# Feed-forward zero's last chunk done for both halves as one seven-product pair, with the top-k rounds, query splits and masks placed anew

## The chip, the cores and the metric

The kernel runs on one core of a Trainium2 chip, in one launch. The metric is the device time of an execution in microseconds, the median over runs. The core has five engines that run side by side, each through its own list of instructions in order: TensorE (PE) multiplies matrices, VectorE (DVE) and ScalarE (ACT) work element by element, GpSimd (POOL) too, and SyncE (SP) issues the DMA transfers. They wait for each other through semaphores.

## The reference

Two layers over 1024 tokens of 1024 features, all in float32. `channel_mixer` stands behind each layer and is most of the work:

```python
def dsa_attention(...):              # layer 0, with 8 heads, key and value shared
    score = einsum(wi, relu(qi . ki)); score = where(causal, score, -inf)
    _, idx = lax.top_k(score, 256)   # each query attends to its 256 best keys
    ... softmax(q . k over idx) . v
def even_layer(x): return x + concat([a_out, b_out]) @ w_out            # a_out is the attention
def odd_layer(x):                    # layer 1: conv module
    z = rms_norm(x) @ w_pw1; y = z[..., :1024] * sigmoid(z[..., 1024:])
    y = causal_depthwise_conv(y, w_dw, width=31) + b_dw
    return x + silu(rms_norm(y)) @ w_pw2
def channel_mixer(x, g, w1, w2):     # 1024 -> 4096 -> 1024, behind each layer
    return x + square(relu(rms_norm(x, g) @ w1)) @ w2
```

## The kernel before, in words

Activations lie transposed: 128 features on the partitions, tokens along the free axis. The sequence is worked on in two halves of 512 tokens (`xt0`, `xt1`), so a matmul has a 128x128 weight block and 512 columns. A float32 product is made of three matmuls: both operands are split into a high part (fp32r) and a low part (the rest), and `products` (L916, L917, L918) adds high·high, high·low and low·high in PSUM.

A **unit** is one output tile of 128 features for one half: 8 weight blocks, so 24 matmuls. Its 512 KB of weights are loaded by SP, split by ACT (high part, L1631) and POOL (low part, L1291), three units ahead of PE. `STAGES` is the order of units: the output projection of half 0 (`wout`), feed-forward zero of half 0 (64 units: four chunks of eight up and eight down), the second attention (tiles 4 to 7 of 128 queries) with `wout` of half 1 behind it, pointwise one of half 0, feed-forward zero of half 1 (64 units), pointwise one of half 1, pointwise two and the first chunk of feed-forward one for each half. In an up unit DVE makes relu(psum) times the norm's factor (`relu_scaled`, L2599), ACT squares it into the high part (L1913, L1915), POOL takes the low part (L1437). In a down unit DVE adds the result to x (`add_residual`, L2420).

The other three chunks of feed-forward one run last, in **a paired session**: both halves are one 2x2 block product with the weights, done with seven products in place of eight (`A11, A12, S1, S2, S3, A22, S4`, a scheme of Strassen and Winograd). A product has 4 steps of 12 matmuls (L1265 to L1267). Around them ACT splits weights and activations (`split_weights`, `split_activations`), DVE takes their low parts (`low_weights`, `low_activations`) and forms the sums of blocks that the scheme needs (`sum_weights`, `sum_activations`), and DVE or ACT reads each product out of PSUM (`read_hidden`, `read_output`, `copy_product`). The session's inputs are the two halves normalised (`normalise_inputs`, L2538, L2541), copied ahead by ACT (`keep_second`, L1945).

**Top-k** of a tile is 32 rounds of MAX8 (the eight largest, L2242) and MATCH_REPLACE8 (mark them, L2247) over its scores, on DVE; tile t has 128(t+1) scores a query. Instructions of one tile's rounds wait for each other through `topk_step`; two tiles are interleaved. Tiles (4, 7) are done in the first two chunks of feed-forward zero of half 0, (5, 6) in the last two, one round of both a unit (`more_topk`, L2602). `mask` (L2302) then turns marks into a bias. The second attention has 32 slots (32 to 63), one for each tile and head: PE makes the scores (L1067, L1068), DVE adds the bias and takes the minimum (L2312), ACT the exponential (L1688), PE transposes (L941) and multiplies with the values (L1091). There DVE also splits the next tile's queries (L2271) and makes its mask.

The norm of a stage needs the mean square over all features: ACT squares (L1528), DVE sums and splits the sum, PE multiplies with a matrix of ones (`mean_of`, L929, L930), ACT takes the root, DVE the reciprocal (L2074 to L2076). The taps of the convolution of half 0 run on DVE in 48 units of feed-forward zero of half 1 (`convolve`, L2443).

## Time and profile before

| what | value |
|---|---|
| runs | 2084.3, 2081.86, 2080.52 us; median 2081.86 |
| the profiled execution: its span | 2078.6 us (its own time is given as this span alone) |
| PE busy | 2049.6 us in 9690 matmuls |
| DVE, ACT, POOL busy | 1493.3, 940.3, 938.2 us |
| chain that ended last | PE 87%, DVE 2%, ACT 1% |
| feed-forward zero of half 0 (PE) | from 332.4 to 683.7 |
| second attention, then `wout` of half 1 | to 829.8 |
| pointwise one of half 0, feed-forward zero of half 1 | to 917.5, to 1266.6 |
| paired session at the end | from 1684 to 2075.4 |

The span is from the first to the last instruction that the profiler shows. The page gives busy time for each engine and the chain of waits; windows give it for one stretch; the timeline lists single instructions, with the idle time before each and what ended it in brackets; groups put instructions of one line and shape together.

### The profile page before, as it was taken

The numbers are of one execution on the slowest core, as the hardware profiler recorded it, in microseconds if no ns is written. First come the engines' busy times: TensorE is split into PE (matmuls) and PEld (weight loads), VectorE is DVE, ScalarE is ACT, GpSimd is POOL, SyncE is SP. The second block draws the span as 40 slices with busy tenths as digits, with TensorE's granted clock in tenths as the row PEclk, the third lists the DMA queues.
The fourth block names the chain that finished last, engine by engine and source line by source line (L and its number), as shares of the span: only waits on it lengthen the run. The fifth ranks groups of instructions, "written<-read, shape, count | busy, mean of one in ns | idle before, by whom it ended". The sixth has DMA issues, their size and how long they took to land.

```text
span 2078.6 us, 29271 instructions
## 1 busy us (share of the span) xinstructions
PE 2049.6 (99%) x9690; PEld 1715.7 (83%) x9690; DVE 1493.3 (72%) x2216; ACT 940.3 (45%) x1390; POOL 938.2 (45%) x595
## 2 busy tenths in 40 slices
PE   7999899999999999999999999999999999999999
PEld 7788788888888898888888888888878888888887
DVE  6698758888888443257777634889954587979877
ACT  6644665232323663343323245444365346464562
POOL 5865674554655003556556456857664700000000
PEclk9999999999999999999999999999999999999999
DMA  6321122332323012223233222333353453434433
GB/s 213 93 70 62 45 69 81 104 95 96 102 92 101 11 54 81 92 82 111 92 102 93 100 92 91 103 101 132 122 177 106 162 205 119 162 131 141 148 128 122
DMA packets 77281, 222.62 MB, mean 107 GB/s; under 512 B 7520, under 2 KB 7904, under 8 KB 76128
## 3 DMA queue, kind: packets, MB, share of 16 engines
q1 hardware_dynamic: 73552, 214.60, 31.4%
q10 hardware_dynamic: 3600, 6.32, 0.8%
q8 instruction: 78, 1.28, 0.3%
q14 instruction: 51, 0.42, 0.1%
HBM read 208.31 MB, written 12.58 MB: 106 GB/s over the span
## 4 chain that ended last, share of the span: by engine, by line
PE 87%; DVE 2%; issue 1%; ACT 1%; POOL 0%; DMA 0%; ACTq 0%; DVEq 0%; POOLq 0%
PE psum L916 20%; PE psum L918 20%; PE psum L917 20%; PE psum L1267 6%; PE psum L1266 6%; PE psum L1265 6%; PE psum L1091 3%; PE psum L941 2%; PE psum L1067 1%; PE psum L1068 1%; DVE psum L2443 1%; PE psum L998 0%; POOL w_buf L1291 0%; DMA raw<-weights 0%; PE psum L1008 0%
## 5 line engine op out<-in xcount | busy, mean ns | idle before, releaser
L1291 POOL TENSOR_TENSOR w_buf<-raw,w_buf 128x1024 fp32r<-128x1024 f32 x250 | 607.5, 2431 | 459.8 <-ACT w_buf L1631 438.4
L1631 ACT ACTIVATE w_buf<-raw 128x1024 fp32r<-128x1024 f32 x236 | 248.5, 1054 | 325.7 <-PE psum L918 264.8
L916 PE MATMUL psum<-hid_buf,w_buf 128*128 128x512 f32 x896 | 350.1, 391 | 0.0
L918 PE MATMUL psum<-hid_buf,w_buf 128*128 128x512 f32 x896 | 349.3, 390 | 0.0
L917 PE MATMUL psum<-hid_buf,w_buf 128*128 128x512 f32 x896 | 349.3, 390 | 0.0
L918 PE MATMUL psum<-h_buf,w_buf 128*128 128x512 f32 x896 | 349.1, 390 | 0.0
L916 PE MATMUL psum<-h_buf,w_buf 128*128 128x512 f32 x896 | 349.1, 390 | 0.0
L917 PE MATMUL psum<-h_buf,w_buf 128*128 128x512 f32 x896 | 349.1, 390 | 0.0
L2443 DVE SCALAR_TENSOR_TENSOR psum<-y_buf,wdw,psum 128x512 f32<-128x512 f32 x435 | 295.0, 748 | 0.0
L1265 PE MATMUL psum<-hid_buf,w_buf 128*128 128x512 f32 x576 | 224.4, 390 | 0.0
L1266 PE MATMUL psum<-hid_buf,w_buf 128*128 128x512 f32 x576 | 224.4, 390 | 0.0
L1267 PE MATMUL psum<-hid_buf,w_buf 128*128 128x512 f32 x576 | 224.4, 390 | 0.0
L918 PEld LDWEIGHTS psum<-hid_buf,w_buf 128*128 128x128 f32 x896 | 168.3, 188 | 35.3
L918 PEld LDWEIGHTS psum<-h_buf,w_buf 128*128 128x128 f32 x896 | 168.3, 188 | 34.9
L916 PEld LDWEIGHTS psum<-h_buf,w_buf 128*128 128x128 f32 x896 | 168.3, 188 | 34.8
L917 PEld LDWEIGHTS psum<-h_buf,w_buf 128*128 128x128 f32 x896 | 168.3, 188 | 34.8
L916 PEld LDWEIGHTS psum<-hid_buf,w_buf 128*128 128x128 f32 x896 | 168.4, 188 | 34.6
L917 PEld LDWEIGHTS psum<-hid_buf,w_buf 128*128 128x128 f32 x896 | 168.5, 188 | 34.4
L2420 DVE TENSOR_TENSOR xt<-xt,psum 128x512 f32<-128x512 f32 (+1 forms) x112 | 76.7, 686 | 125.7 <-PE psum L918 124.1
L2247 DVE MATCH_REPLACE8 score<-small,score 128x640 f32<-128x640 f32 (+5 forms) x176 | 158.2, 905 | 0.0
L2242 DVE MAX8 small<-score 128x8 f32<-128x640 f32 (+5 forms) x176 | 153.8, 911 | 2.6 <-ACT b_tok L1583 2.2
L1913 ACT ACTIVATE s_ring<-t_ring 128x512 f32<-128x512 f32 x80 | 50.6, 632 | 226.6 <-DVE t_ring L2599 226.6
(318 smaller groups left out, 3350.4 us busy)
## 6 DMA issues: line engine op xcount, KB each, us to landing
raw<-weights SPq DMA_DIRECT2D x312, 512.0 KB, 3.5
w_more<-weights SPq DMA_DIRECT2D x48, 512.0 KB, 4.3
xt<-x_t SPq DMA_DIRECT2D x2, 2048.0 KB, 8.4
out_t<-xt SPq DMA_DIRECT2D x16, 256.0 KB, 2.0
x_in<-x_t SPq DMA_DIRECT2D x12, 256.0 KB, 6.6
m_kept<-m_ring ACTq DMA_DIRECT2D x12, 256.0 KB, 2.0
c_kept<-c_ring ACTq DMA_DIRECT2D x12, 256.0 KB, 2.7
m_in<-m_kept SPq DMA_DIRECT2D x3, 1024.0 KB, 7.1
```

Source lines behind the costliest of these rows:

```text
L916: nc.tensor.matmul(acc, lhs_hi, rhs_hi, start=first, stop=False)
L917: nc.tensor.matmul(acc, lhs_hi, rhs_lo, start=False, stop=False)
L918: return nc.tensor.matmul(acc, lhs_lo, rhs_hi, start=False, stop=last)
L1265: nc.tensor.matmul(acc, hi, hid_buf[:, 0, k, :], start=start, stop=False, skip_group_check=True)
L1266: nc.tensor.matmul(acc, hi, hid_buf[:, 1, k, :], start=False, stop=False, skip_group_check=True)
L1267: mm = nc.tensor.matmul(acc, lo, hid_buf[:, 0, k, :], start=False, stop=j == 3, skip_group_check=True)
L1291: nc.gpsimd.tensor_tensor(dst_lo, src, dst_hi.bitcast(F32), ALU.subtract).then_inc(done, 1)
L1631: nc.scalar.activation(w_buf[:, 0, :, slot * P:(slot + 1) * P], raw[:, slot % 2], ACT.Copy).then_inc(hi_up, 1)
L2242: V.max(top8[z], score[tiles[z]][:]).then_inc(topk_step, 1)
L2247: V.match_replace(out=s, in_to_replace=top8[z], in_values=s, imm_value=TAKEN).then_inc(topk_step, 1)
L2420: V.tensor_tensor(x, x, psum[:, r, :], ALU.add).then_inc(unit_read, 1)
L2443: ins = V.scalar_tensor_tensor(out=c_buf[:, ct, :] if k == CONV - 1 else acc, in0=yflat(ct, k), scalar=wdw[:, ct, k:k + 1], in1=acc, op0=A ...
```

## The change

The last chunk (q = 3) of feed-forward zero is taken out of both halves' stages (48 units each are left) and done for both halves together in a session of its own, behind `wout` of half 1 and ahead of pointwise one of half 0: 14 products, since all seven are made in the up stage as well. For it the inputs of feed-forward zero are needed twice: x of half 0 is saved to DRAM ahead of that stage and loaded again into `h_first`, x of half 1 is saved ahead of the session and loaded into `h_first` in its last product but a few, as input of feed-forward zero of half 1. The statistics of half 1 are made in the session (`mean_of` at its third step). ACT and DVE make the input of pointwise one in the session's last 14 steps (`early_input`).

Top-k of tiles 4 to 7 gets a new order over 46 units in place of 64: 32 rounds of (4, 5), 19 of (6, 7), 13 of tile 6 alone, spread by their cost. The last 13 rounds of tile 7 (26 steps) go into slots 34 to 54 of the second attention. GpSimd splits the queries and makes the masks of tiles 5 to 7, and DVE waits for the mask at a tile's first head. Half 0's convolution taps start in pointwise one (5 units without, then 3, then 5 a unit) and run at 6 a unit in feed-forward zero of half 1. GpSimd takes the first low parts of the session.

The core of the diff (waits, tiles and SP's loads mostly left out):

```diff
-SOLO = 1
+SOLO0, SOLO = 3, 1
-STAGES = [("wout", 0, WOUT, 8), ("ff0", 0, FF0, 64), ("wout", 1, WOUT, 8), ("pw1", 0, PW1, 16),
-          ("ff0", 1, FF0, 64), ("pw1", 1, PW1, 16),
+STAGES = [("wout", 0, WOUT, 8), ("ff0", 0, FF0, 16 * SOLO0), ("wout", 1, WOUT, 8), ("pw1", 0, PW1, 16),
+          ("ff0", 1, FF0, 16 * SOLO0), ("pw1", 1, PW1, 16),
+ROUNDS_67 = 19
+LATE_GROUPS = [(4, 5)] * ROUNDS + [(6, 7)] * ROUNDS_67 + [(6,)] * (ROUNDS - ROUNDS_67)
+LATE_SLOTS = {**{a: 1 for a in range(34, 55) if a not in (42, 50)}, **{a: 2 for a in (36, 37, 43, 45, 51, 53, 54)}}
+def late_groups_at(u, end):
+    cost = [sum(t + 1.5 for t in tiles) for tiles in LATE_GROUPS]
+    at = [sum(cost[:n + 1]) * end / sum(cost) for n in range(len(cost))]
+    return [tiles for tiles, when in zip(LATE_GROUPS, at) if u < when <= u + 1]
+LATE_STEPS = [(t, take) for tiles in LATE_GROUPS for take in range(2) for t in tiles]
+LATE_STEPS += [(7, take) for _ in range(ROUNDS - ROUNDS_67) for take in range(2)]
 PRODUCTS = [(n, term) for n in range(PAIRED_STAGES) for term in range(TERMS)
+            if n % 2 or n < 2 * EARLY_PAIRS or term not in (A11, A12)]
+EARLY_INPUT_AT = (14, 13, 12, 11, 6, 5, 4, 3)
+PW1_TAPS = ([0] * 5 + [3] * 3 + [5] * 8, [0] * 4 + [4] * 4 + [6] * 8)
+FF0_TAPS = [6] * 16 * (SOLO0 - 1) + [4, 3] + [0] * 14
...
 # TensorE
+            def pair_products(session):
+                for g in range(SESSION[session], SESSION[session + 1]):
+                    v, term, p = g // 4, term_of(g), g % 4
+                    if g == 2:
+                        mean_of("ff0_1", sum_lo)
+                    pe.wait_ge(w_lo, g // 2 + 1)
...
 # GpSimd
+            def split_queries(t):
+                pool.wait_ge(q_split, t)
+                pool.wait_ge(tr_up, TR["q", t - 1, 1] + 1)
+                stack, q = stack_of(t), q_tok[:, t]
+                link(nc.gpsimd.tensor_scalar(q, q, -(HD ** -0.5), None, ALU.mult))
+                link(nc.gpsimd.tensor_copy(stack[:, :, 0, :], q))
+                T(stack[:, :, 1, :], q, stack[:, :, 0, :].bitcast(F32), ALU.subtract).then_inc(q_split, 1)
+            def mask(t):
+                pool.wait_ge(topk_step, late_steps_through(t))
+                nc.gpsimd.tensor_scalar(score[t][:], score[t][:], 0.9 * TAKEN, -NEG, ALU.is_gt, ALU.mult
+                                        ).then_inc(late_mask, 1)
+                elif (name, half) == ("wout", 1):
+                    for t in range(5, 8):
+                        split_queries(t)
+                        mask(t)
+                    units(first, 8, last=True)
+                    for m in range(3):
+                        first_low_weights(m)
+                    for z in range(2):
+                        first_low_activations(1, z)
+                    first_low_weights(3)
...
 # ScalarE
-                    units(first, 8, again(0, "pw1_0", G_OD, h_buf))
+                    units(first, 8, both(square_second(first), keep_second(G_FF0), split_first), last=True, unrolled=True)
+                    pair_splits(0)
+            def split_first(i, r):
+                if i and r % 2:
+                    split_activations(0, r // 2)
+            def pair_splits(session):
+                first, end = SESSION[session], SESSION[session + 1]
+                for m in range(first // 2, first // 2 + W_AHEAD // 2):
+                    split_weights(m)
+                    if session == 0 and m:
+                        split_activations(1, m - 1)
...
 # VectorE
+            def late_topk(count):
+                for n in range(late_done[0], late_done[0] + count):
+                    t, take = LATE_STEPS[n]
+                    before, s = late_step_before(n), score[t][:]
+                    wait_apart(dve, topk_step, STEPS_01 + (0 if before is None else before + 1), passed_v)
+                    if take:
+                        ins = V.match_replace(out=s, in_to_replace=top8[t % 2], in_values=s, imm_value=TAKEN)
+                    else:
+                        ins = V.max(top8[t % 2], s)
+                    ins.then_inc(topk_step, 1)
+                late_done[0] += count
 # in attention_slot
+                if t > 4 and h == 0:
+                    dve.wait_ge(late_mask, t - 4)
+                if a in LATE_SLOTS:
+                    late_topk(LATE_SLOTS[a])
 # in feed-forward zero of half 0
+                            for tiles in late_groups_at(u, 16 * SOLO0 - 2):
+                                late_topk(2 * len(tiles))
+                            if u == 16 * SOLO0 - 2:
+                                mask(4)
+                                attention_slot(32, 1)
+            def early_input(k):
+                n = KT * PREP["pw1_0"] + k
+                prep_low(n, k, flat(xt[0], None, k), h_buf, G_OD)
+                add_squares(KT * SUM["pw1_0"] + k, k % 2, sq_sum[:])
+            def pair_sums(session):
+                first, end = SESSION[session], SESSION[session + 1]
+                if session == 0:
+                    split_sums("ff0_1")
+                    norm_of("ff0_1", rms_second)
+                    for k in range(4):
+                        normalise_second(k, rms_second)
+                for g in range(first, end):
+                    v, p = g // 4 + 1, g % 4
+                    if session == 0 and g in (5, 6):
+                        normalise_second(2 * g - 6, rms_second)
+                        normalise_second(2 * g - 5, rms_second)
...
```

## Rows read from the trace of the kernel before

**Rows 1.** The page: busy time of each engine; the chain by engine

```profile
PE 2049.6 (99%) x9690; PEld 1715.7 (83%) x9690; DVE 1493.3 (72%) x2216; ACT 940.3 (45%) x1390; POOL 938.2 (45%) x595
...
PE 87%; DVE 2%; issue 1%; ACT 1%; POOL 0%; DMA 0%; ACTq 0%; DVEq 0%; POOLq 0%
```

**Rows 2.** Windows: us, busy PE, PEld, DVE, ACT, POOL; clock, DMA share, GB/s

```profile
427.00:514.00 87.00, 87.00 (x386) 72.12 (x385) 73.25 (x114) 26.24 (x32) 48.48 (x24) 1.00 0.30 97
683.70:783.80 100.10, 98.56 (x784) 92.70 (x783) 44.28 (x86) 65.85 (x139) 0.00 (x0) 1.00 0.08 29
```

**Rows 3.** Timeline, PE and DVE, first units of feed-forward zero: start, duration

```profile
332.43 0.40 PE L916 MATMUL psum<-h_buf,w_buf 128*128 128x512 f32 x1
...
344.49 0.69 DVE L2599 SCALAR_TENSOR_TENSOR t_ring<-psum,rms_bc 128x512 f32<-128x512 f32 x1 [0.33 <-DVE rms_bc L2076]
...
348.94 0.68 DVE L2599 SCALAR_TENSOR_TENSOR t_ring<-psum,rms_bc 128x512 f32<-128x512 f32 x1
```

**Rows 4.** Groups by shape, top-k on DVE: busy us, mean ns, idle

```profile
L2242 DVE MAX8 small<-score 128x8 f32<-128x1024 f32 x32 | 38.7, 1209 | 0.0
L2242 DVE MAX8 small<-score 128x8 f32<-128x896 f32 x32 | 34.4, 1075 | 0.0
L2242 DVE MAX8 small<-score 128x8 f32<-128x768 f32 x32 | 30.4, 950 | 0.0
L2242 DVE MAX8 small<-score 128x8 f32<-128x640 f32 x32 | 26.2, 819 | 0.0
```

**Rows 5.** Timeline, last relu of an up stage to its low part

```profile
426.51 0.69 DVE L2599 SCALAR_TENSOR_TENSOR t_ring<-psum,rms_bc 128x512 f32<-128x512 f32 x1 [0.79 <-PE psum L918]
...
428.99 1.30 POOL L1437 TENSOR_TENSOR hid_buf<-s_ring,hid_buf 128x512 f32 x1 [4.37 <-ACT hid_buf L1915]
```

**Rows 6.** Timeline, DVE: one round of tile 3 alone

```profile
209.06 0.68 DVE L2242 MAX8 small<-score 128x8 f32<-128x512 f32 x1
...
210.78 0.69 DVE L2242 MAX8 small<-score 128x8 f32<-128x512 f32 x1
```

**Rows 7.** Timeline, DVE, end of feed-forward zero; group of ACT's exponentials

```profile
677.57 0.69 DVE L2420 TENSOR_TENSOR xt<-xt,psum 128x512 f32<-128x512 f32 x1 [0.91 <-PE psum L918]
678.18 0.49 DVE L2302 TENSOR_SCALAR score<-score 128x640 f32<-128x640 f32 x1
...
L1688 ACT ACTIVATE p_buf<-s_buf,small 128x640 f32<-128x640 f32 x8 | 6.6, 828 | 5.5 <-DVE small L2312 5.1 <-PE psum L941 0.3
```

**Rows 8.** Second attention, L2312 on DVE: a slot; idle before it, times

```profile
698.68 0.82 DVE L2312 CUSTOM_DVE_ANT_0 s_buf<-psum,score 128x640 f32<-128x640 f32 x1 [1.53 <-PE psum L1068]
...
  PE psum L1068: 42.8, 24
```

**Rows 9.** Groups by shape: ACT's squares and weight splits, POOL's low parts

```profile
L1528 ACT ACTIVATE sq_ring<-xt 128x512 f32<-128x512 f32 x24 | 14.8, 617 | 0.0
L1631 ACT ACTIVATE w_buf<-raw 128x1024 fp32r<-128x1024 f32 x236 | 248.5, 1054 | 325.7 <-PE psum L918 264.8 <-DMA raw<-weights 34.4 <-DVE m_ring L2561 16.7
L1291 POOL TENSOR_TENSOR w_buf<-raw,w_buf 128x1024 fp32r<-128x1024 f32 x250 | 607.5, 2431 | 459.8 <-ACT w_buf L1631 438.4 <-ACT w_buf L1538 20.3 <-POOL q_tok L1318 0.5
```

**Rows 10.** Timeline, PE: from the output projection into pointwise one

```profile
829.54 0.39 PE L918 MATMUL psum<-hid_buf,w_buf 128*128 128x512 f32 x1
829.76 0.39 PE L916 MATMUL psum<-h_buf,w_buf 128*128 128x512 f32 x1
```

**Rows 11.** Timeline, DVE and POOL: half 1 normalised, beside weight splits

```profile
1640.86 10.41 DVE L2538 TENSOR_TENSOR h_second<-h_second,rms_bc 128x512 f32<-128x512 f32 x8
...
1644.46 5.65 POOL L1291 TENSOR_TENSOR w_buf<-raw,w_buf 128x1024 fp32r<-128x1024 f32 x2
```

**Rows 12.** Timeline, PE: the first matmuls after a long stop

```profile
10.79 0.69 PE L916 MATMUL psum<-hid_buf,h_buf 128*128 128x424 f32 x1 [7.58 <-DVE h_buf L2088]
...
14.11 0.43 PE L916 MATMUL psum<-hid_buf,h_buf 128*128 128x424 f32 x1
...
14.57 0.36 PE L918 MATMUL psum<-hid_buf,h_buf 128*128 128x424 f32 x1
```

More of the change, by code:

```diff
@@ L506, in build @@
         x_kept = nc.dram_tensor("x_kept", (P, KT, HALF), F32)
+        x_early = [nc.dram_tensor(f"x_early{half}", (P, KT, HALF), F32) for half in range(2)]
         m1_kept = nc.dram_tensor("m1_kept", (P, 4 * PRE, HALF), F32)
@@ L1182, in mlp @@
                     if q == 0:
-                        units(first, 8, operand, prep_lo, KT * PREP[name], mean=(name, sum_lo))
+                        units(first, 8, operand, prep_lo, KT * PREP[name],
+                              mean=None if (stage, half) == ("ff0", 1) else (name, sum_lo))
                     else:
@@ L1194, in mlp @@
                     mean = None
-                    if q == 3 and (stage, half) == ("ff0", 1):
+                    if q == chunks_of(stage)[-1] and (stage, half) == ("ff0", 1):
                         mean = ("conv0", sum_lo)
@@ L1922, in mlp @@
                         continue
-                    if q == 3 and (stage, half) == ("ff0", 1):
+                    if q == chunks_of(stage)[-1] and (stage, half) == ("ff0", 1):
                         squares = conv_squares(0)
-                    units(first + 16 * q, 8, both(hidden_hi, squares), mean=None if q else name_of(stage, half))
+                    units(first + 16 * q, 8, both(hidden_hi, squares), unrolled=squares is not None,
+                          mean=None if q or (stage, half) == ("ff0", 1) else name_of(stage, half))
                     if (stage, half) == ("ff1", 1):
@@ L2618, in mlp @@
                         continue
-                    if conv and not late and q < 3:
+                    if (stage, half) == ("ff0", 0):
+                        residual = add_residual(down, half)
                         for r in range(16):
-                            done = 16 * q + r
+                            u = 16 * q + r
+                            if u == 16 * SOLO0 - 8:
+                                split_queries(4)
                             if r < 8:
@@ L2641, in mlp @@
                             clear_sum(psum[:, 7, :])
-                        if (stage, half) == ("ff0", 0):
-                            split_queries(4)
-                            residual, rounds = add_residual(down, half), more_topk(1)
-                            units(down, 4, residual, rounds)
-                            for r in range(4):
-                                residual(1, r)
-                                if r < 2:
-                                    rounds(1, r)
-                                if r == 2:
-                                    mask(4)
-                                    attention_slot(32, 1)
-                            continue
                         if (stage, half) == ("ff1", 1):
```

618 lines of the change are left out of this document (381 added, 237 removed).

## The prediction, made before the change was run

> **What bounds the kernel now.** I read the page first: TensorE (PE) is busy 99% of the span and holds 87% of the chain that ended last [rows 1], so time leaves the kernel only with matmuls, and enters it wherever PE is made to wait. Then the windows by stage: in a stretch of feed-forward zero PE works without a gap and a matmul costs 87.00/386 = 0.2254 us, while VectorE (DVE) is busy 84% of it, with top-k rounds; in the second attention DVE is busy 44% [rows 2]. Last the timelines at the places where the change puts a new chain in front of PE. Each instruction's own time comes from the groups by shape.
>
> **PE's matmuls.** The last chunk of feed-forward zero costs 2 halves × 16 units × 24 = 768 matmuls before, and 14 products × 4 steps × 12 = 672 as a pair. 96 × 0.2254 = **−21.6**. Everything below is what has to be paid for it.
>
> **First chunk of feed-forward zero, half 0.** DVE starts its first relu 12.1 us after PE's first matmul of the stage (344.49 against 332.43) [rows 3]. Before, relu and a (4,7) round take 348.94 − 344.49 = 4.45 of a unit's 24 × 0.2265 = 5.44 us, so DVE gains 1 us a unit on PE. The round's share is 4.45 − 0.61 = 3.84, against 2 × (0.819 + 1.209) = 4.06 of the four instructions [rows 3, 4]: interleaved rounds run at 0.946 of their sum. After, the first 23 units hold 32 rounds of (4,5): 2 × (0.819 + 0.950) × 0.946 = 3.35 each, 1.39 a unit, with the relu 5.3 of 5.44. The backlog hardly drains. At the turn from the up to the down matmuls DVE is about 2.5 late; the chain from the last relu to the low part of the hidden tile takes 430.29 − 426.51 = 3.78 [rows 5], and the last tile is wanted 7 × 3 × 0.2265 = 4.76 after the turn. 2.5 + 3.78 − 4.76 = **+1.5** (0 if the backlog drains as before, 4 if it doesn't at all). Later turns find it smaller.
>
> **Tail of that stage.** Units 40 to 45 hold one (6,7) round, 13 rounds of tile 6 alone, and 6 relu or residual steps. A lone round is a chain: MAX8, MATCH_REPLACE8, MAX8 on one score tile. The one such row is tile 3, 512 wide: 210.78 − 209.06 = 1.72, where two instructions at the interleaved rate would be 2 × 0.680 × 0.946 = 1.29 [rows 4, 6]. So +0.43 of waiting a round, and tile 6 alone costs 2 × 1.075 × 0.946 + 0.43 = 2.46. 13 × 2.46 + 4.32 + 6 × 0.61 + 1.4 (splitting queries of tile 4) = 41.4. DVE can't begin with them before PE ends unit 40, 41 × 5.44 = 223.0 into the stage, so it is done at 264.4. (Over the whole stage: 12.1 + 32 × 3.35 + 19 × 4.32 + 13 × 2.46 + 46 × 0.61 + 1.4 = 263, about the same: there is no slack left anywhere.) Behind that stand unit 46's residual 0.61, mask 0.5 and masked minimum 0.82, then ScalarE's exponential 0.83 and 0.1 for hops [rows 7, 8], before PE may go on with slot 32's probabilities: 267.3, where its units end at 48 × 5.44 = 261.1. **+6.1** (0 to 8: nothing if lone rounds run at the interleaved rate; 8 if the first chunk's backlog is still there).
> Here the Trainium skill speaks against me: "VectorE: DVE Perf Modes", section "The DRAIN you can't avoid", says that the pipeline is emptied after each VectorE instruction anyway and that a semaphore between chained ones costs nothing extra. By it this term would be 0.5. The row shows otherwise, so the rule is only a rival.
>
> **Second attention.** 13 rounds of tile 7, lone too, are 26 steps of 1.21 = 31.5 us [rows 4], in slots 34 to 54. DVE waits there 42.8 us for scores, 24 times [rows 8]: 1.8 a slot. A slot with one step fits. Seven slots have two, 2.42, of which some 0.85 goes past the wait; the slots' probabilities lie about 0.4 ahead of PE. I take 0.3 for each of seven, **+2.0** (0 to 6, all of 7 × 0.85). GpSimd's splits and masks are off DVE there. Its mask of 1024 has no row; bounds are DVE's own of 640, 0.49 [rows 7], and GpSimd's two-input subtraction of 1024, 2.43 [rows 9]; I take 1.6 (one input), and even 2.43 with the split before it fits the two slots (6 us) between tile 7's last step and its first masked minimum. So zero; were it late, DVE would stand at a tile's first minimum, and everything of that slot behind it.
>
> **Start of the paired chunk.** Before, PE passes from the output projection into the next stage without a gap (829.54, 829.76) [rows 10], since the weights of the next units were split ahead. After, ScalarE first ends the last unit's work: residual 0.69 on DVE, square 0.617 and a scaled copy of the same size; then half of the first activations 1.054, the first weights' high part 1.054, and GpSimd's low part 2.43 [rows 7, 9], with hops of 0.3 in all: **+6.8** of PE standing (5.5 if the copy falls behind the split, 7.5 with longer hops).
>
> **S1, the third product.** Its right-hand side needs half 1 normalised. The mean can only be made after PE's first two steps (5.4 into the session), then root and norm, 4 normalisations of the second half, the subtraction and its two splits, all in DVE's order among its weight sums. The eight normalisations in the row took 10.41/8 = 1.30 each, beside GpSimd's subtraction, where DVE's residual of the same size takes 0.69 [rows 7, 11]. That order puts the low part of S1's second half about 36.3 after the projection's end; PE wants it at 6.8 + 8 steps × 2.72 + half a step 1.36 + the mean's own matmuls 0.4 = 30.3. In two waits (2.2 and 3.9) **+6.1** (0 if the statistics come as early as the weights, 3.3 without GpSimd's hold on DVE, 9 if sums wait too).
>
> **End of the paired chunk.** The input of pointwise one is made in its last 14 steps; DVE gets 8 subtractions and 8 sums more there and is about 0.8 late for the last reads: **+0.8** (0 to 3). Pointwise one starts with three weight units split ahead, so no gap there. Feed-forward zero of half 1 gets six taps a unit, 6 × 0.69 + 0.61 = 4.7 of 5.44: zero. The 2 MB moves lie on SyncE's queue in front of weight units that have two slots of slack: zero; were one late, it would show as a wait of ScalarE for a load.
>
> **Clock.** The granted clock is 1.00 in every stretch [rows 2], the higher of the two levels (1.2 and 2.4 GHz). After PE stood 7.58 us early in the kernel, nine matmuls of 424 columns took 14.11 − 10.79 = 3.32, 0.37 each, and the next two 14.57 − 14.11 = 0.46, 0.23 each [rows 12]: about 9 × 0.14 = 1.3 us at the lower level. The new stop of 6.8 can bring one such; **+1.0** (0 to 5: three more stops).
>
> **Sum:** −21.6 + 1.5 + 6.1 + 2.0 + 6.8 + 6.1 + 0.8 + 1.0 = +2.7. From the profiled span of 2078.6, 2081.3; the runs' median, 2081.86, lies 3.3 above that span, so 2084.6, told as 2084.5. This kernel's measurement can tell 0.2%, 4.2 us, from no change; +2.7 is inside it.
>
> **Rivals.**
> *Lone rounds cost no more than interleaved ones.* For it: the row of a lone round is one of few, of another tile, and from a stretch with other work. Against: 1.72 beside 1.29 [rows 6]. The tail's 6.1 falls by 13 × 0.43 = 5.6, and 2084.5 to 2079. (The Trainium skill's section on the DRAIN, named above, says this.)
> *DVE keeps up.* The (4,5) backlog drains, the tail fits, and S1's operands come in time: for it, DVE is idle 16% of the stage's stretch [rows 2], and half of the normalisations may run beside an idle GpSimd at 0.69 rather than 1.30. Against: the two sums over units above. −21.6 + 0 + 1 + 1 + 6.8 + 2 + 0.8 + 0 = −10, so 2072.
> *The second attention becomes DVE's* (the other side). Place: slots 34 to 54. A slot's steps stand behind its minimum and in front of the next one; where a step isn't ready (it waits for the one before it, lone) or a slot is shorter than 0.82 + 1.21 and PE's 0.4 of lead is used up, each of 19 slots pays: 7 × 0.85 + 12 × 0.2 = 8.4 rather than 2.0. It decides from the first slot whose scores PE must hold back. For it: tile 4's slots come every 1.53 + 0.82 = 2.35 us [rows 8], and one step leaves 0.3 of that. Against: 42.8 of waiting for 31.5 of work. 2091.
>
> **Chances.** The forecast .42, its own range 2078 to 2088 (.34 of it within 0.2%, .08 slower); lone rounds free .10 (half within, half faster); DVE keeps up .20 (faster); the second attention, or as many repeated cold starts, .28 (slower). Faster .25, same .39, slower .36. The range 2071 to 2094 holds all four cases' middles and leaves the joint extremes out.
>
> **What would show it.** In the profile after: 96 matmuls fewer at an unchanged pitch; DVE idle almost nowhere between 345 and 590; a PE gap near 6 us before slot 32's values, ended by an exponential; a gap near 7 us between the projection and the first paired matmul, ended by GpSimd's weights; two gaps before S1, ended by VectorE; a few slots of under 1 us. I am wrong if DVE idles in the tail, if PE reaches S1 later than its operands, or if PE waits in a stage that I put at zero (pointwise one's start, half 1's feed-forward zero).

## The result, and the profile after

The changed kernel takes 2087.4 us (median of 11 runs, 2085.6 to 2089.1), the kernel before 2081.7 (11 runs): a ratio of 1.0028, 95% interval 1.0020 to 1.0036. It is slower by 5.7 us, more than the 0.2% from which the forecast told a change. The forecast was 2084.5, in the range 2071 to 2094.

The page of the changed kernel, busy time by engine:

```profile
PE 2040.1 (98%) x9594; PEld 1704.9 (82%) x9594; DVE 1603.8 (77%) x2314; ACT 972.0 (47%) x1420; POOL 876.0 (42%) x565
```

9690 − 9594 = 96 matmuls are gone, as computed, and with them 21.8 us of PE's time at the pitch of 0.2267 (a unit of 24 in 5.44); but its busy time falls by only 9.5 [rows 1], and beside it stand stops. The stops, from the timeline of PE (start, duration, in brackets the idle time and what ended it):

```profile
602.40 0.76 PE L1069 MATMUL psum<-ident,p_buf 128*128 128x128 f32 x5 [3.48 <-ACT p_buf L1865]
676.47 0.95 PE L1069 MATMUL psum<-ident,p_buf 128*128 128x128 f32 x7 [0.69 <-ACT p_buf L1865]
759.19 0.80 PE L1376 MATMUL psum<-b_first,w_buf 128*128 128x512 f32 x1 [6.66 <-POOL w_buf L1561]
788.57 0.80 PE L1376 MATMUL psum<-hid_buf,w_buf 128*128 128x512 f32 x1 [3.12 <-DVE hid_buf L2712]
901.28 0.50 PE L1376 MATMUL psum<-hid_buf,w_buf 128*128 128x512 f32 x1 [2.23 <-DVE hid_buf L2712]
1016.71 0.70 PE L1044 MATMUL psum<-hid_buf,w_buf 128*128 128x512 f32 x1 [2.43 <-DVE hid_buf L2303]
```

In order: slot 32's probabilities (the tail), tile 7's first slot, the start of the paired chunk, S1, A22 at the end of the chunk, and the first unit of half 1's feed-forward zero. "Half clock" below is time at the lower of the two levels. Where the kernel before has no gap at all [rows 10], there are 6.66 us. The second half of the loss is not idle time. Windows of the changed kernel (columns as in [rows 2]), first a full-speed stretch, then those behind five of the stops:

```profile
466.00:509.00 43.00, 43.00 (x192) 35.59 (x191) 40.98 (x59) 9.88 (x11) 23.71 (x11) 1.00 0.31 98
602.40:612.00 9.60, 9.44 (x45) 8.50 (x45) 5.99 (x12) 4.32 (x11) 0.78 (x1) 0.64 0.01 3
759.20:764.00 4.80, 4.80 (x11) 3.80 (x12) 0.00 (x0) 2.14 (x3) 4.80 (x3) 0.50 0.53 167
788.60:792.00 3.40, 3.40 (x9) 2.74 (x10) 3.40 (x5) 0.52 (x1) 0.00 (x0) 0.57 0.04 11
901.30:906.00 4.70, 4.70 (x21) 3.88 (x22) 4.08 (x5) 1.81 (x2) 0.00 (x0) 1.00 0.08 30
1016.70:1021.00 4.30, 4.29 (x12) 3.38 (x13) 4.27 (x8) 0.74 (x1) 2.38 (x1) 0.60 0.01 4
```

PE is busy the whole of each stretch, with half as many matmuls as time: 11 in 4.80 us behind the start's stop, at a granted clock of 0.50 (the 1.2 GHz level), where 4.80/0.2267 = 21 fit at 2.4 GHz. Time lost is the stretch times one minus the clock: 3.5 + 2.4 + 1.5 + 1.7 = 9.1 us.

The account of this execution: −21.8 + stops (3.5 + 0.7 + 6.7 + 3.1 + 2.2 + 2.4 = 18.6) + half clock 9.1 = +5.9, beside +5.7 between the medians. The smaller stops nearly cancel: over these stages they add up to 1.8 here, and the kernel before stood 2.1 there. This execution is the slowest of the eleven; its span, 2087.3, lies 8.7 above the profiled 2078.6, of which 2.3 is there when feed-forward zero starts (334.70 below, 332.43 in [rows 3]), so 6.4 is to be set beside the 5.9.

Readings that the steps below need, from the timeline of the changed kernel. PE's first matmul of feed-forward zero, then lone rounds of tile 6 and VectorE's minimum of slot 32:

```profile
334.70 0.40 PE L1044 MATMUL psum<-h_buf,w_buf 128*128 128x512 f32 x1
...
592.05 1.09 DVE L2465 MAX8 small<-score 128x8 f32<-128x896 f32 x1
593.29 0.09 DVE L2463 MATCH_VALUE_LOAD score<-small,score 128x8 f32 x1 [0.15 <-DVE small L2465]
593.37 1.07 DVE L2463 MATCH_REPLACE8 score<-small,score 128x896 f32<-128x896 f32 x1
594.59 1.09 DVE L2465 MAX8 small<-score 128x8 f32<-128x896 f32 x1
...
600.56 0.82 DVE L2543 CUSTOM_DVE_ANT_0 s_buf<-psum,score 128x640 f32<-128x640 f32 x1
```

A lone round takes 594.59 − 592.05 = 2.54, with waits of 0.15 between its steps; the minimum stands 265.9 behind PE's first matmul. The first turn of that stage from up to down units (PE's first down matmul, VectorE's last relu, GpSimd's last low part):

```profile
379.53 0.39 PE L1044 MATMUL psum<-hid_buf,w_buf 128*128 128x512 f32 x1
...
380.43 0.68 DVE L2845 SCALAR_TENSOR_TENSOR t_ring<-psum,rms_bc 128x512 f32<-128x512 f32 x1
...
382.74 1.29 POOL L1603 TENSOR_TENSOR hid_buf<-s_ring,hid_buf 128x512 f32 x1 [0.24 <-ACT hid_buf L2089]
```

Two units of pointwise one on VectorE, from one read of PSUM to the next but one:

```profile
989.73 0.68 DVE L3037 TENSOR_TENSOR s_ring<-psum,rms_bc 128x512 f32<-128x512 f32 x1
991.73 1.39 DVE L2303 SCALAR_TENSOR_TENSOR hid_buf<-h_first,gain,hid_buf 128x512 fp32r<-128x512 f32 x1 [1.31 <-ACT hid_buf L1699]
...
1001.51 0.68 DVE L3037 TENSOR_TENSOR s_ring<-psum,rms_bc 128x512 f32<-128x512 f32 x1
```

And GpSimd's mask of tile 7, with VectorE waiting for it:

```profile
669.53 3.65 POOL L1556 TENSOR_SCALAR score<-score 128x1024 f32<-128x1024 f32 x1 [26.23 <-DVE score L2463]
...
673.34 1.22 DVE L2543 CUSTOM_DVE_ANT_0 s_buf<-psum,score 128x1024 f32<-128x1024 f32 x1 [2.90 <-POOL score L1556]
```

### The profile page after: what moved, and what is told of

Same layout as the page of the kernel before. It is cut to its first block, busy times and chain, and to the rows that moved or that the text cites. A ratio compares the mean times of both kernels' runs of the same rounds, so it can differ in the third digit from the quotient of the medians.

```text
span 2087.3 us, 28431 instructions
## 1 busy us (share of the span) xinstructions
PE 2040.1 (98%) x9594; PEld 1704.9 (82%) x9594; DVE 1603.8 (77%) x2314; ACT 972.0 (47%) x1420; POOL 876.0 (42%) x565
## 3 DMA queue, kind: packets, MB, share of 16 engines
q8 instruction: 77, 1.26, 0.2%
## 4 chain that ended last, share of the span: by engine, by line
PE 53%; DVE 3%; issue 1%; ACT 0%; DMA 0%; POOL 0%; ACTq 0%; DVEq 0%
PE psum L1044 11%; PE psum L1046 11%; PE psum L1045 11%; PE psum L1378 7%; PE psum L1376 7%; PE psum L1377 7%; DVE psum L2679 1%; DVE hid_buf L2303 1%; PE psum L1343 0%; PE psum L1345 0%; PE psum L1347 0%; DVE psum L2696 0%; DMA raw<-weights 0%; ACT hid_buf L1699 0%; DVE s_ring L3037 0%
## 5 line engine op out<-in xcount | busy, mean ns | idle before, releaser
L1433 POOL TENSOR_TENSOR w_buf<-raw,w_buf 128x1024 fp32r<-128x1024 f32 x218 | 529.4, 2431 | 483.2 <-ACT w_buf L1808 461.3
L1808 ACT ACTIVATE w_buf<-raw 128x1024 fp32r<-128x1024 f32 x204 | 214.5, 1053 | 246.5 <-PE psum L1046 179.9
L1376 PE MATMUL psum<-hid_buf,w_buf 128*128 128x512 f32 x784 | 305.9, 390 | 5.4 <-DVE hid_buf L2712 5.4
L1378 PE MATMUL psum<-hid_buf,w_buf 128*128 128x512 f32 x784 | 305.5, 390 | 0.0
L1377 PE MATMUL psum<-hid_buf,w_buf 128*128 128x512 f32 x784 | 305.5, 390 | 0.0
L1044 PE MATMUL psum<-hid_buf,w_buf 128*128 128x512 f32 x768 | 300.6, 391 | 2.4 <-DVE hid_buf L2303 2.4
L1045 PE MATMUL psum<-hid_buf,w_buf 128*128 128x512 f32 x768 | 299.7, 390 | 0.0
L1046 PE MATMUL psum<-hid_buf,w_buf 128*128 128x512 f32 x768 | 299.6, 390 | 0.0
L1046 PE MATMUL psum<-h_buf,w_buf 128*128 128x512 f32 x768 | 298.8, 389 | 0.0
L1044 PE MATMUL psum<-h_buf,w_buf 128*128 128x512 f32 x768 | 298.8, 389 | 0.0
L1045 PE MATMUL psum<-h_buf,w_buf 128*128 128x512 f32 x768 | 298.8, 389 | 0.0
L1376 PEld LDWEIGHTS psum<-hid_buf,w_buf 128*128 128x128 f32 x784 | 147.5, 188 | 36.7 <-DVE hid_buf L2712 6.2
L1377 PEld LDWEIGHTS psum<-hid_buf,w_buf 128*128 128x128 f32 x784 | 147.6, 188 | 30.9
L1378 PEld LDWEIGHTS psum<-hid_buf,w_buf 128*128 128x128 f32 x784 | 147.4, 188 | 30.6
L1044 PEld LDWEIGHTS psum<-hid_buf,w_buf 128*128 128x128 f32 x768 | 144.6, 188 | 32.7 <-DVE hid_buf L2303 2.9
L1046 PEld LDWEIGHTS psum<-hid_buf,w_buf 128*128 128x128 f32 x768 | 144.6, 188 | 30.6
L1045 PEld LDWEIGHTS psum<-hid_buf,w_buf 128*128 128x128 f32 x768 | 144.7, 188 | 29.8
L1044 PEld LDWEIGHTS psum<-h_buf,w_buf 128*128 128x128 f32 x768 | 144.1, 188 | 30.1
L1046 PEld LDWEIGHTS psum<-h_buf,w_buf 128*128 128x128 f32 x768 | 144.2, 188 | 30.0
L1045 PEld LDWEIGHTS psum<-h_buf,w_buf 128*128 128x128 f32 x768 | 144.1, 188 | 29.9
L2463 DVE MATCH_REPLACE8 score<-small,score 128x640 f32<-128x640 f32 (+3 forms) x128 | 128.4, 1010 | 0.0
```

The costliest lines, as they stand in the source:

```text
L1044: nc.tensor.matmul(acc, lhs_hi, rhs_hi, start=first, stop=False)
L1045: nc.tensor.matmul(acc, lhs_hi, rhs_lo, start=False, stop=False)
L1046: return nc.tensor.matmul(acc, lhs_lo, rhs_hi, start=False, stop=last)
L1376: nc.tensor.matmul(acc, hi, b_split(v, 0, j), start=start, stop=False, skip_group_check=True)
L1377: nc.tensor.matmul(acc, hi, b_split(v, 1, j), start=False, stop=False, skip_group_check=True)
L1378: mm = nc.tensor.matmul(acc, lo, b_split(v, 0, j), start=False, stop=j == 3, skip_group_check=True)
```

## The experiments

Each was timed against the kernel before in the same session, with 5 to 11 runs; ratios are to that kernel, with a 95% interval. Times are to be held against 2087.4.

**e_mean: the statistics of half 1 earlier.** On PE and on ScalarE:

```diff
-                    if g == 2:
+                    if g == 0:
                         mean_of("ff0_1", sum_lo)      # and root_of on ScalarE
```

> The changed kernel, but with the mean of half 1 (TensorE) and its root (ScalarE) ahead of the paired chunk's first step and not of its third. Theory (the stop before S1 hangs on the statistics, which wait for TensorE's own third step while VectorE stands still for 9 us): the stop of 3.3 us before S1 goes, and with it the half clock of the eight matmuls behind it, 1.7: 2087.4 - 5.0 = 2082.4. Rival (VectorE's order of weight sums and splits ahead of S1 decides): the stop stays at 2 to 3, and the time at 2086 to 2087.

2085.7 (1.0019, 1.0010 to 1.0028). The stop before S1 stays at 2.75, so the theory fell, though not for the rival's reason. VectorE, GpSimd and PE's stop before S1 in this run's timeline:

```profile
763.63 8.41 DVE L2771 TENSOR_TENSOR h_second<-h_second,rms_second 128x512 f32<-128x512 f32 x4
...
762.87 5.21 POOL L1566 TENSOR_TENSOR hid_buf<-h_first,hid_buf 128x1024 fp32r<-128x1024 f32 x2
768.03 2.85 POOL L1561 TENSOR_TENSOR w_buf<-w_more,w_buf 128x1024 fp32r<-128x1024 f32 x1
...
787.19 0.78 PE L1376 MATMUL psum<-hid_buf,w_buf 128*128 128x512 f32 x1 [2.75 <-DVE hid_buf L2712]
```

and in the changed kernel:

```profile
770.62 2.80 DVE L2771 TENSOR_TENSOR h_second<-h_second,rms_second 128x512 f32<-128x512 f32 x4
...
763.77 4.92 POOL L1566 TENSOR_TENSOR hid_buf<-h_first,hid_buf 128x1024 fp32r<-128x1024 f32 x2
768.66 2.40 POOL L1561 TENSOR_TENSOR w_buf<-w_more,w_buf 128x1024 fp32r<-128x1024 f32 x1
```

The normalisations begin 7 us earlier (1 of it this execution's own, as the start's stop ends at 758.1 for 759.2) and take 8.41 in place of 2.80: they end at 772.0, 1.2 behind GpSimd's last low part, and in the changed kernel at 773.4. What was won ahead was lost beside GpSimd. Counted from the end of the output projection, PE goes on with S1 after 35.57 (787.19 − 751.62) in this run and after 36.04 (788.57 − 752.53) in the changed kernel.

**e_port: the six first low parts on VectorE.** e_mean, and

```diff
                     units(first, 8, last=True)            # GpSimd
-                    for m in range(3):
-                        first_low_weights(m)
-                    for z in range(2):
-                        first_low_activations(1, z)
-                    first_low_weights(3)
...
                     split_sums("ff0_1")                   # VectorE
+                    low_weights(0)
+                    for z in range(2):
+                        low_weights(1 + z)
+                        low_activations(1, z)
                     norm_of("ff0_1", rms_second)
...
-                        if g > 1:
-                            low_weights((g - 1 + W_AHEAD) // 2)
+                        low_weights((g - 1 + W_AHEAD) // 2)
```

> The changed kernel with the mean of half 1 ahead of the first step, as in the run before with the early mean (2085.7; there four normalisations took 8.41 us beside GpSimd's low parts, where they had taken 2.80 after them), and besides VectorE makes the paired chunk's six first low parts in place of GpSimd. Theory (GpSimd's low parts hold VectorE's two-input instructions until they are done, 20 us after the projection's end, and so decide when S1's operands come): four normalisations take 2.8, the stop before S1 (3.1 to 3.3) goes with the half clock behind it: 2087.4 - 5.0 = 2082.4; TensorE's stop at the start stays near 6.9. Rival (VectorE's own work decides; it gets 6 x 1.2 = 7.3 us more): the stop before S1 stays at 2 or more, 2086 to 2088.

2081.5 (0.9999, 0.9990 to 1.0008). VectorE's normalisations, and PE's stops before S1 and in S2:

```profile
764.09 2.50 DVE L2766 TENSOR_TENSOR h_second<-h_second,rms_second 128x512 f32<-128x512 f32 x4
...
783.15 0.50 PE L1376 MATMUL psum<-hid_buf,w_buf 128*128 128x512 f32 x1 [0.38 <-DVE hid_buf L2707]
...
795.31 0.50 PE L1376 MATMUL psum<-hid_buf,w_buf 128*128 128x512 f32 x1 [0.99 <-DVE hid_buf L2707]
```

2.50 for four, although they start at the same point as in e_mean; what is gone beside them is GpSimd. VectorE has 7.3 us more to do, and S1's stop falls from 2.75 in e_mean to 0.38 (a new one of 0.99 in S2 stands beside that); no half clock follows them. PE goes on with S1 33.29 behind the projection's end. This is shown, since the two runs differ only in the engine that makes them: GpSimd's low parts set when S1's operands come. By the Trainium skill's "SBUF — State Buffer", section "Who interferes with whom", a VectorE instruction with two inputs in SBUF contends with a GpSimd instruction that reads SBUF; 8.41 beside 2.50 agrees.

**e_start: the first splits ahead of the projection's last unit.**

```diff
-                if i and r % 2:
-                    split_activations(0, r // 2)
+                if i and r in (1, 2):
+                    split_activations(0, r - 1)
+                if i and r == 2:
+                    split_weights(0)
+                    split_weights(1)
...
+                    if session or m > 1:
                         split_weights(m)
...
-                        if m >= 6:
-                            low_activations(0, m - 6)
+                        if m == 6:
+                            low_activations(0, 0)
+                            low_activations(0, 1)
```

> The changed kernel, but ScalarE splits the first two weight pairs and the first activations ahead of its work on the projection's last unit, so that the low parts are ready when the projection ends. Theory (the stops add up, since the statistics of half 1 hang on TensorE's own third step and move with it): the stop of 6.8 at the start of the paired chunk falls under 1 and the half clock behind it (2.6) goes; S1's stop stays near 3.3: 2087.4 - 9 = 2078. Rival (S1's operands are bound to the projection's end, whenever TensorE starts): the stop before S1 grows by what the start gave, to 9 or 10, and only 1 to 3 us are won: 2085.

2081.9 (1.0004, 0.9995 to 1.0013): 5.5 of the 9 that adding up would give. PE's stops, and VectorE's normalisations:

```profile
750.63 0.50 PE L1376 MATMUL psum<-b_first,w_buf 128*128 128x512 f32 x1 [1.26 <-POOL w_buf L1561]
...
760.01 5.42 DVE L2775 TENSOR_TENSOR h_second<-h_second,rms_second 128x512 f32<-128x512 f32 x4
...
775.47 0.76 PE L1376 MATMUL psum<-hid_buf,w_buf 128*128 128x512 f32 x1 [2.30 <-DVE hid_buf L2716]
...
780.59 0.50 PE L1376 MATMUL psum<-hid_buf,w_buf 128*128 128x512 f32 x1 [2.22 <-DVE hid_buf L2716]
```

The start's stop falls from 6.66 to 1.26, the two before S1 grow from 3.12 to 4.52. Both theories hold in part: about a quarter of the win comes back.

**e_warm: matmuls in the stop.** It adds 28 matmuls, whose result the next product overwrites.

```diff
+                    if g == 0:
+                        pe.wait_ge(unit_read, UNITS_BEFORE[0] - 3)
+                        pe.wait_ge(b_hi, 1)
+                        for _ in range(28):
+                            nc.tensor.matmul(product_bank(0), b_first[:, 0, 0, 0:P], b_first[:, 0, 0, :], start=True,
+                                             stop=True, skip_group_check=True)
```

> The changed kernel, with 28 matmuls more, of 512 columns, written to a PSUM bank that the next product overwrites, in TensorE's stop between projection and paired chunk. They take 6.3 us of the 6.8 and nothing waits for them. Theory (the twelve matmuls behind the stop at 0.43 us, at a granted clock of 0.50, are real time): the granted clock there is 1.00, the time 2087.4 - 2.6 = 2084.8. Rival (S1's stop is bound to the projection's end and takes up what the clock gives): clock 1.00, but S1's stop grows by 1 to 2.6 and the time stays within 1 us of 2087.4.

2087.3 (1.0029, 1.0018 to 1.0039): no change, the rival's figure. The window behind the start; the projection's last matmul and PE's stops before S1; VectorE's normalisations:

```profile
758.30:763.00 4.70, 4.61 (x20) 3.84 (x21) 0.00 (x0) 3.72 (x5) 4.70 (x3) 1.00 0.57 159
```

```profile
751.27 0.39 PE L1046 MATMUL psum<-hid_buf,w_buf 128*128 128x512 f32 x1
...
782.56 0.47 PE L1382 MATMUL psum<-hid_buf,w_buf 128*128 128x512 f32 x1 [1.63 <-DVE hid_buf L2718]
...
787.68 0.79 PE L1382 MATMUL psum<-hid_buf,w_buf 128*128 128x512 f32 x1 [3.49 <-DVE hid_buf L2718]
...
767.47 5.07 DVE L2777 TENSOR_TENSOR h_second<-h_second,rms_second 128x512 f32<-128x512 f32 x4
```

20 matmuls in place of 11, clock 1.00: with PE kept at work there is no half clock. The 2.4 us come back before S1, whose stops grow from 3.12 to 5.12. In the changed kernel the half clock at the start was therefore free: S1 would have waited anyway. PE goes on with S1 787.68 − 751.66 = 36.02 behind the projection's end, as in the changed kernel (36.04): the normalisations begin 2.3 earlier, counted from there, and take 5.07 in place of 2.80.

**e_taps: eight taps later.**

```diff
-PW1_TAPS = ([0] * 5 + [3] * 3 + [5] * 8, ...)
-FF0_TAPS = [6] * 16 * (SOLO0 - 1) + [4, 3] + [0] * 14
+PW1_TAPS = ([0] * 5 + [3] * 3 + [4] * 8, ...)
+FF0_TAPS = [6] * 16 * (SOLO0 - 1) + [6, 6, 3] + [0] * 13
```

> The changed kernel, but eight convolution taps moved from pointwise one's last eight units (4 a unit in place of 5) to the end of half 1's feed-forward zero. Theory: the stop of 2.6 us in the first unit of that feed-forward, where the eighth normalised tile is late behind five taps, goes, and so does the half clock behind it (nine matmuls, 2.0): 2087.4 - 4.6 = 2082.8. If the half clock in the rows costs no time: 2084.8. Rival (the taps only carry the lateness to the last chunk): 2087.

2083.2 (1.0008, 0.9999 to 1.0017), −4.2, near the theory with the half clock counted. The window of that stage's first units, without a stop, and from the changed kernel one of the subtractions that its taps stood beside:

```profile
1005.00:1020.00 15.00, 15.00 (x68) 12.43 (x67) 12.72 (x18) 4.53 (x6) 7.91 (x5) 1.00 0.34 107
```

```profile
1008.72 1.37 DVE L2303 SCALAR_TENSOR_TENSOR hid_buf<-h_first,gain,hid_buf 128x512 fp32r<-128x512 f32 x1
```

**e_end: pointwise one's input later.**

```diff
-EARLY_INPUT_AT = (14, 13, 12, 11, 6, 5, 4, 3)
+EARLY_INPUT_AT = (10, 9, 8, 7, 6, 5, 4, 3)
```

> The changed kernel with the first four tiles of pointwise one's input made 10 to 7 steps ahead of the paired chunk's end and not 14 to 11. Theory (the stop of 2.4 us before A22, the last product but one, comes from these subtractions and sums standing in VectorE's queue ahead of A22's low parts): it goes, 2087.4 - 2.4 = 2085, or 2084 where a half clock followed it. Rival (VectorE is full over the whole stretch): the stop only moves, before S4 or into pointwise one, 2087.

2083.3 (1.0009, 1.0000 to 1.0018), −4.1: the stop before A22 is gone, and no other comes between it and pointwise one. It gave more than the 2.2 of the stop; behind that same stop the profiles of e_mean, e_start, e_taps, e_bal and f_session show clocks of 0.59 to 0.64 over 4 to 5 us, those of the changed kernel, e_warm, e_port and e_dve 1.00, so a half clock in some executions is the likely rest; it is not shown.

**e_bal: fewer lone rounds.** 5 rounds of tile 6 and 9 of tile 7 in the second attention, 4 lone ones ahead of it.

```diff
-ROUNDS_67 = 19
-LATE_GROUPS = [(4, 5)] * ROUNDS + [(6, 7)] * ROUNDS_67 + [(6,)] * (ROUNDS - ROUNDS_67)
-LATE_SLOTS = {**{a: 1 for a in range(34, 55) if a not in (42, 50)}, **{a: 2 for a in (36, 37, 43, 45, 51, 53, 54)}}
+ROUNDS_67, LATE_6 = 23, 5
+LATE_GROUPS = [(4, 5)] * ROUNDS + [(6, 7)] * ROUNDS_67 + [(6,)] * (ROUNDS - ROUNDS_67 - LATE_6)
+LATE_SLOTS = {**{a: 1 for a in range(33, 55)}, **{a: 2 for a in (43, 45, 47, 51, 53, 54)}}
+LATE_STEPS += [(6, take) for _ in range(LATE_6) for take in range(2)]
```

> The changed kernel with another split of the top-k rounds: 32 rounds of (4,5), 23 of (6,7) and only 4 of tile 6 alone in feed-forward zero of half 0, and in the second attention 5 rounds of tile 6 and 9 of tile 7 (28 steps for 26). VectorE's work in feed-forward zero falls by 13 x 2.5 + 19 x 4.3 - 4 x 2.5 - 23 x 4.3 = 5 us. Theory (the stop of 3.6 us before slot 32's values is VectorE's lateness, and the half clock in the slots behind it, 0.65 over 10 us, costs about 3): the stop falls under 0.5, the slots run at full clock: 2087.4 - 6 = 2081. Rival (the second attention then becomes VectorE's, with two more steps and no free slot): the stop goes, but its slots lose 3 to 6 us: 2084 to 2087.

2087.2 (1.0029, 1.0018 to 1.0039): no change. PE's stops at the tail and three slots on:

```profile
597.93 0.76 PE L1070 MATMUL psum<-ident,p_buf 128*128 128x128 f32 x5 [1.23 <-ACT p_buf L1866]
605.29 0.33 PE L1070 MATMUL psum<-ident,p_buf 128*128 128x128 f32 x1 [1.62 <-ACT pt_buf L1815]
```

The tail falls from 3.48 to 1.23, and the clock behind it is 1.00, but slots that had none now stop. PE's stops up to tile 7's first slot add up to 5.5 in this profile and 5.4 in the changed kernel: what the tail gave, the slots took, as the rival said. That the half clock's 3.5 doesn't show in the median either stays open. In this profile some of it came back elsewhere: over the 10 us behind S1's stop the clock was 0.72 (0.85 in the changed kernel), over the 10 us behind A22's 0.83 (1.00).

**e_dve: queries and masks back on VectorE.**

```diff
-                    for t in range(5, 8):                # GpSimd
-                        split_queries(t)
-                        mask(t)
...
-                if t > 4 and h == 0:                     # VectorE
-                    dve.wait_ge(late_mask, t - 4)
-                if h == Q_AT - 3 and t < 3:
+                if h == Q_AT - 3 and t % 4 < 3:
                     split_queries(t + 1)
-                if h == 7 and t < 3:
+                if h == 7 and t % 4 < 3:
                     mask(t + 1)
```

> The changed kernel with the queries of tiles 5 to 7 split and their masks made by VectorE, in the slots where the kernel before did it, and not by GpSimd. It adds three times some 1.4 + 0.6 = 6 us to VectorE in the second attention. Theory (VectorE's late rounds leave little there): the slots lose 2 to 5 us, 2089 to 2092. Rival (42.8 us of idle time for 31.5 us of steps leave room): within 1 us of 2087.4, and GpSimd's part of the change was worth nothing.

2092.2 (1.0049, 1.0035 to 1.0062): +4.8, as the theory had it. GpSimd's part is worth it in spite of its slow mask. In the profiles PE needs 153.47 from slot 32's values to the projection's end, for 150.13 in the changed kernel, with 996 matmuls in both: it stands 3.1 for 2.0, and is busy 150.4 for 148.1, so two thirds of the loss here are half clock and not waiting.

**f_session, f_most, f_all, f_last: toward a version that beats both.** f_session has e_start's splits, `low_weights(0)` on VectorE behind them and the other first low parts there ahead of the norm, with PE's mean where it was and ScalarE's root a step earlier:

```diff
+                            low_weights(0)               # at m == 6
...
+                    for z in range(2):                   # behind split_sums
+                        low_weights(1 + z)
+                        low_activations(1, z)
+                    low_weights(3)
```

> The run with VectorE making the first low parts (2081.5), and besides the early first splits (alone 2081.9): first two weight pairs and first activations split by ScalarE ahead of the projection's last unit, their low parts made by VectorE there, the mean again ahead of the third step, the root a step earlier on ScalarE. Theory (the start's stop and S1's are both bound to the projection's end by the same chain of first low parts; off GpSimd it is short enough for both): start under 0.5, S1's stops under 2 in all, no half clock: 2087.4 - 6.8 - 2.6 - 2.5 = 2075.5. Rival (VectorE's own chain binds S1 to the projection's end): what the start gives, up to 6.4, comes back before S1: 2080 to 2082.

2080.1 (0.9992, 0.9983 to 1.0001). The start's stop is 0.1, but S1's are 1.43 and 3.49: nearest to the rival. f_most adds e_taps and e_end:

> The run before, and with it the taps moved (alone 2083.2, -4.2) and pointwise one's input made later (alone 2083.3, -4.1). Theory (the stops lie in different stages and add up): 2075.5 - 8.3 = 2067, 14 under the kernel before. Rival (the median is not a sum of stops; part of the half clock counted in each is one execution's chance): 2070 to 2072.

2074.4 (0.9962, 0.9949 to 0.9976), −5.7 and not −8.3. f_all moves 3 rounds of tile 6 into the second attention, in exchange for 3 of tile 7:

```diff
+ROUNDS_67, LATE_6 = 22, 3
```

> The run before, and with it 22 rounds of (6,7), 7 of tile 6 alone, and in the second attention 3 rounds of tile 6 and 10 of tile 7: the same 26 steps in the same slots as the change, 1.9 us less of VectorE ahead of slot 32. Theory: the stop of 3.6 before slot 32's values falls to 1.7 and the half clock behind it (about 3) goes in most executions: 2 to 5 under the run before. Rival (as with 28 steps: what the stop gives, the slots lose): within 1 us of the run before.

2072.8 (0.9958, 0.9944 to 0.9971), no change that can be told from f_most. The theory failed: the stop before slot 32's values is 3.32, for 3.47 in f_most.

```profile
599.97 1.33 PE L1070 MATMUL psum<-ident,p_buf 128*128 128x128 f32 x5 [3.32 <-ACT p_buf L1861]
```

f_last puts S1's two low parts one behind the other:

```diff
+                        if g == 5:
+                            low_activations(v, 0)
+                            low_activations(v, 1)
+                            dve.wait_ge(product_up, g + 1)
+                            read_hidden(g)
...
-                    if session == 0 and g in (5, 6):
+                    if session == 0 and g in (7, 8):
                         normalise_second(...)
```

> The fastest run so far (2072.8), with VectorE's order ahead of S1 changed: both low parts of S1's activations one behind the other, then the read of the sixth product step, and the last four normalisations of half 1 (2 x 1.28 us) only behind them, where S2's sums need them. Theory (the two stops left before S1, 1.6 and 3.7, are VectorE's order: 5 us of other work between its two low parts): both fall under 1 and the half clock behind them goes: 2072.8 - 4 to - 6 = 2067 to 2069. Rival (VectorE is full from the projection's end to S2, so what is put off is late there): the stops move to S1's later steps or to S2: within 1.5 us of 2072.8.

2070.8 (0.9949, 0.9935 to 0.9962), the fastest, though its interval overlaps that of f_all: 16.6 under the change, 10.8 under the kernel before. Two windows of the paired chunk, and the stops that are left in the second:

```profile
740.00:775.00 35.00, 34.64 (x152) 28.02 (x151) 30.69 (x35) 18.02 (x22) 0.00 (x0) 1.00 0.51 180
775.00:800.00 25.00, 20.78 (x90) 16.30 (x89) 23.52 (x23) 18.06 (x24) 0.00 (x0) 1.00 0.41 138
```

```profile
784.21 0.47 PE L1377 MATMUL psum<-hid_buf,w_buf 128*128 128x512 f32 x1 [2.28 <-DVE hid_buf L2712]
...
787.53 0.50 PE L1377 MATMUL psum<-hid_buf,w_buf 128*128 128x512 f32 x1 [1.71 <-DVE hid_buf L2712]
```

The start and S1 run through; VectorE, busy 23.52 of 25.00, is late for S2 now. What is put off there is late there, as the rival said, but less: S1's 4.9 (1.44 and 3.49 in f_all) are gone and S2's 4.0 came. Its clock was 1.00 behind all of its stops, the tail's 3.33 too, which no other profile with a tail above 3 shows; so a part of the 2.0 under f_all may be this execution's chance.

## Why the prediction was right or wrong

The range held the time and the sign of the sum was right; its size was half the measured one, by terms that miss in both directions: together they were 8.5 too high (first chunk, tail, second attention, start, S1) and 11.9 too low (end of the chunk, pointwise one, clock). That the time came out within 3 us is in part luck.

| term | forecast | profile after |
|---|---|---|
| 96 matmuls | −21.6 | −21.8 |
| first chunk | +1.5 | 0 |
| tail | +6.1 | 3.5 |
| second attention | +2.0 | 0.7 |
| start | +6.8 | 6.7 |
| S1 | +6.1 | 3.1 |
| end of the chunk | +0.8 | 2.2 |
| pointwise one into half 1 | 0 | 2.4 |
| half clock | +1.0 | 9.1 |

- **Clock: the step that failed.** "The new stop of 6.8 can bring one such" counted one restart, of 1.3 us. Four of six stops had one. The one behind S1's stop (9 matmuls in 3.40, 1.5 lost) was like the row; the other three cost 1.7, 2.4 and 3.5, and what makes them longer is not shown. My bound of 5 was too low as well. But the 9.1 isn't all a loss that mending brings back: e_warm shows that the start's 2.4 is paid by S1's wait either way.
- **96 matmuls:** the count was right; 87.00/386 takes in the matmuls that the window's edges cut, so the pitch of 0.2254 was 0.5% short.
- **Start:** right, by its own chain, down to the releaser (GpSimd's low part).
- **Tail:** VectorE came when forecast: its minimum 265.9 after PE's first matmul of the stage, where the sum had 264.4 + 0.61 + 0.5 = 265.5, and PE went on 267.7 after it, for 267.3. The lone round was 2.54 against 2.46, so the row of tile 3 carried over. The stop was 3.5 and not 6.1 because PE's side of the subtraction was too small: 48 × 5.44 left out the mean, the transposes of tile 4's queries and slot 32's scores, some 3 us. f_all adds that the order counts and not the stage's total: with 1.9 us less of work on VectorE the last three units still held two, two and three lone rounds, as in f_most, and the stop stayed. The Trainium skill ("VectorE: DVE Perf Modes", section "The DRAIN you can't avoid") measured that a semaphore after each of a row of VectorE copies costs nothing extra. If that held here, a lone round would take 2 × 1.075 × 0.946 = 2.03, an estimate; the trace's 2.54 is against it: a step that waits for the one before it starts 0.15 after its end, while interleaved rounds run at 0.946 of their sum [rows 3, 4].
- **First chunk:** no stop, by a narrow margin. VectorE's last relu began 0.90 behind the turn (380.43 − 379.53) and not 2.5; its low part was done at 4.50 (382.74 + 1.29 − 379.53), wanted at 4.76. The 2.5 had no working, and the sum's own numbers give more: 12.1 + 7 × 5.27 = 49.0, where the turn is at 8 × 5.44 = 43.5. Measured, the last relu stood 45.7 behind PE's first matmul: seven units held nine rounds and took 4.85 each, for 5.27.
- **S1:** VectorE's side came as forecast, PE's did not. PE went on 36.04 behind the projection's end, for 36.3; it had wanted the operand at 32.9 (788.57 − 3.12 − 752.53) and not at 30.3, since the half clock at the start had taken 2.4. So 2.4 of the clock's 9.1 stood in the forecast under S1's name. That the 36 held is partly luck: PE's mean came 2.4 later than forecast, by that half clock, and the four normalisations, most of them behind GpSimd's last low part, took 2.80 and not 4 × 1.30. e_mean and e_warm bring the mean forward and win 0.5 and nothing; e_port shows that GpSimd's hold is the cause. I had S1's term and the start's added as if they were independent. They share one chain from the projection's end: in e_warm, e_taps, e_end, e_bal and e_dve S1 goes on 36.02 to 36.07 behind it, and in e_start, where GpSimd begins earlier, 31.22.
- **End of the chunk:** right place and cause (e_end), 2.2 for 0.8.
- **Pointwise one into half 1, put at zero:** wrong; the prediction had named a wait there as a sign of being wrong. I counted six taps a unit behind it and not the five beside the making of its input. Two units took VectorE 1001.51 − 989.73 = 11.78, where PE takes 2 × 5.44 = 10.88: ten taps, two reads of PSUM, two subtractions of 1.4 beside GpSimd's work, and a wait of 1.31 for ScalarE. So VectorE fell behind by 0.9 every two units. e_taps took it away.
- **Second attention:** room for the steps was there, as forecast; the 0.69 left comes from GpSimd's mask, 3.65 where my bounds ended at 2.43. With smaller stops PE stood 1.9 there without the tail, and 1.5 in the kernel before. The rival "the second attention becomes VectorE's" didn't come; e_dve shows that it lay 6 us of work away. The chances had named "as many repeated cold starts" beside it, and these came.

## What to carry to other kernels

When a change puts a new chain in front of a full TensorE, find the event from which the chain starts and all stops that hang on it: they are one term, and mending the first stop hands part of the win to the next. Price a stop with the half clock that may follow it. Work moved to GpSimd to relieve VectorE can hold up VectorE's two-input instructions where they meet (8.41 for 2.50 here); on this short critical stretch VectorE did better with 7 us more of its own, while in the second attention the move was worth 4.8.

## What the runs showed of the hardware

- The same stop is followed by half clock in one execution and not in another: behind 2.2 us before A22 the clock was 1.00 in the changed kernel and 0.59 in e_mean; behind 2.4 us before half 1's first unit 0.60 in the changed kernel and 1.00 in e_mean. A stop of 6.5 to 6.7 was followed by 0.50 to 0.56 over some 5 us in each of the seven profiles that had one; e_warm's matmuls, whose results nobody reads, kept it away.
- GpSimd's compare and multiply of 128x1024 in float32 took 3.65 us, longer than its subtraction of two such tiles, 2.43 [rows 9].
